# The causal mask of an SSD mixer: a triangle multiplied into the state products and a minimum on VectorE, in place of masking matmuls on TensorE

## The reference, cut to what matters

```python
seg = a_cum[..., :, None] - a_cum[..., None, :]
decay = jnp.where(causal, jnp.exp(jnp.where(causal, seg, 0.0)), 0.0)
cb = jnp.einsum('bclgn,bcsgn->bcgls', cc, bc)
y_diag = jnp.einsum('bcgrls,bcsgrp->bclgrp', cb[:, :, :, None] * decay, xdt)
```

## Time and profile before

| | us |
|---|---|
| median of 3 runs | 1277.57 |
| the runs | 1276.2 to 1277.68 |
| the profiled execution | 1276.93 |
| its span, first to last instruction | 1275.0 |
| TensorE (PE) busy in it | 1254.1 |
| VectorE (DVE) busy | 832.5 |
| ScalarE (ACT) busy | 513.0 |

### The profile page before, as it was taken

One profiled execution on the slowest core, in us unless ns is written; L12 is line 12 of the kernel. 1 busy time (PEld: TensorE's weight loads), 2 busy tenths in 40 slices (PEclk: granted clock), 3 DMA queues, 4 the chain that ended last, 5 costly groups with the idle time before them and its releaser, 6 DMA issues.

```text
span 1275.0 us, 16443 instructions
## 1 busy us (share of the span) xinstructions
PE 1254.1 (98%) x6120; PEld 1011.2 (79%) x6120; DVE 832.5 (65%) x1002; ACT 513.0 (40%) x794; POOL 234.5 (18%) x157
## 2 busy tenths in 40 slices
PE   7999999999999999999999999999999999999997
PEld 6777777777787888888878888888888888888886
DVE  4546646646397546634787777767686777787863
ACT  5435535547675225213433242424232423233441
POOL 0000000052300002610221111111111121212118
PEclk9999999999999999999999999999999999999999
DMA  6101001110004212110211211111111212111113
GB/s 244 50 34 34 33 33 34 33 50 17 1 1 149 67 67 83 66 34 4 80 67 33 67 50 49 49 49 66 39 60 57 67 39 66 33 67 33 66 58 125
DMA packets 22803, 71.93 MB, mean 56 GB/s; under 512 B 2528, under 2 KB 2784, under 8 KB 22752
## 3 DMA queue, kind: packets, MB, share of 16 engines
q1 hardware_dynamic: 22752, 71.22, 16.4%
HBM read 67.02 MB, written 4.19 MB: 56 GB/s over the span
## 4 chain that ended last, share of the span: by engine, by line
PE 68%; DVE 11%; issue 9%; ACT 5%; DMA 3%; POOL 2%; DVEq 1%; SPq 0%; ACTq 0%; POOLq 0%
PE ps L736 14%; PE ps L738 14%; PE ps L737 14%; PE ps L1095 4%; PE ps L1094 4%; PE ps L1093 4%; DVE w_lo L607 3%; DVE conv_ff L1960 2%; PE ps L831 2%; PE ps L814 2%; ACT conv_ff L1518 2%; DMA down_raw<-u_down 2%; DMA raw<-u_up 1%; PE ps L790 1%; ACT w_hi L602 1%
## 5 line engine op out<-in xcount | busy, mean ns | idle before, releaser
L736 PE MATMUL ps<-x_hi,w_hi 128*128 128x512 f32 x336 | 139.3, 414 | 8.5 <-DVE x_lo L1714 7.3
L1093 PE MATMUL ps<-mix_hi,w_hi 128*128 128x512 f32 x352 | 137.1, 389 | 0.9 <-DVE partial L1991 0.9
L1094 PE MATMUL ps<-mix_lo,w_hi 128*128 128x512 f32 x352 | 136.9, 389 | 0.0
L1095 PE MATMUL ps<-mix_hi,w_lo 128*128 128x512 f32 x352 | 136.9, 389 | 0.0
L738 PE MATMUL ps<-x_hi,w_lo 128*128 128x512 f32 x336 | 132.4, 394 | 0.0
L737 PE MATMUL ps<-x_lo,w_hi 128*128 128x512 f32 x336 | 131.9, 393 | 0.0
L2012 DVE TENSOR_TENSOR acc<-acc,ps 128x512 f32<-128x512 f32 x144 | 95.6, 683 | 42.5 <-PE ps L738 42.2
L2279 POOL TENSOR_TENSOR weight_sums<-raw 128x512 f32<-128x512 f32 x22 | 32.0, 1452 | 471.4 <-DMA raw<-u_up 471.4
L736 PE MATMUL ps<-h_hi,w_hi 128*128 128x512 f32 x288 | 113.7, 395 | 1.5 <-DVE acc L2012 0.6
L737 PE MATMUL ps<-h_lo,w_hi 128*128 128x512 f32 x288 | 112.2, 390 | 0.0
L738 PE MATMUL ps<-h_hi,w_lo 128*128 128x512 f32 x288 | 112.1, 389 | 0.0
(11 more groups left out here) (264 smaller groups left out, 2723.1 us busy)
## 6 DMA issues: line engine op xcount, KB each, us to landing
raw<-u_up SPq DMA_DIRECT2D x44, 512.0 KB, 3.3
raw<-u_in SPq DMA_DIRECT2D x22, 512.0 KB, 3.3
down_raw<-u_down SPq DMA_DIRECT2D x38, 256.0 KB, 2.7
x_stage<-u_x SPq DMA_DIRECT2D x8, 512.0 KB, 8.8
raw<-u_out SPq DMA_DIRECT2D x8, 512.0 KB, 3.3
x_nat<-x_nat SPq DMA_DIRECT2D x8, 512.0 KB, 3.3
raw<-u_gate SPq DMA_DIRECT2D x8, 512.0 KB, 3.2
out<-o_norm SPq DMA_DIRECT2D x7, 512.0 KB, 2.6
```

Source lines behind the costliest of these rows:

```text
L736: mm(dst, w_hi, x_hi, start=first, stop=False)
L1093: mm(dst, w_h[:, k], t_h[:, kt, :], start=fresh and kt == 0, stop=False, skip_group_check=True)
L1094: mm(dst, w_h[:, k], t_l[:, kt, :], start=False, stop=False, skip_group_check=True)
L1095: last = mm(dst, w_l[:, k], t_h[:, kt, :], start=False, stop=kt == 3, skip_group_check=True)
```

## The change

The mask leaves TensorE: `mask(h)` and its two tables are gone, and so is the wait of `between(h)` for it. In its place `products(g)` multiplies `cb<g>` by a triangle of ones while it takes it out of PSUM, and it does so on VectorE, not on ScalarE. `decayed(h)` takes the minimum of `decayed` and one before the product with `cb`, so that an exponential above the diagonal can't spoil the zero. VectorE's order around the stage is written anew. `TASKS` and `PAIR_OF` stay as they are. Two small VectorE instructions that made the tables at the kernel's start go too.

```diff
-MASK_BEFORE = {"cu1": 0, "st2": 1, "cb1": 2, "yy0": 3}
-MASK_INSIDE = {4: 4, 6: 5}
...
-        def mask(h):
-
-            eng.wait_ge(cexp_done, h + 1)
-            dst = two(task_place("cu%d" % h)[0])
-            for b in range(2):
-                last = mm(dst[:, b * HALF:(b + 1) * HALF].rearrange("p (k n) -> p k n", k=4), ident_r[:, :],
-                          mask_r[:, :].unsqueeze(1).broadcast_to([P, 4, P]), start=False, stop=True, skip_group_check=True)
-            last.then_inc(masked, 1)
...
-        def products(g):
-            src, free = task("cb%d" % g)
-            act(cb[:, g, :], src, ACT.Copy).then_inc(free, 1)
...
-            act(ce[h][:, :], src, ACT.Exp).then_inc(cexp_done, 1)
+            act(ce[h][:, :], src, ACT.Exp)
...
             src, free = task("cu%d" % h)
-            eng.wait_ge(masked, h + 1)
...
-        products(0)
         between(1)
         from_start(2)
         between(2)
-        products(1)
...
+        def products(g):
+            src, free = task("cb%d" % g)
+            by_tile = lambda ap: ap.rearrange("p (k n) -> p k n", k=MT)
+            v.tensor_tensor(by_tile(cb[:, g, :]), by_tile(src), table("tri_le").unsqueeze(1).broadcast_to([P, MT, P]),
+                            ALU.mult).then_inc(free, 1)
...
-            v.tensor_tensor(wt[h][:, :], wt[h][:, :], cb[:, g, :], ALU.mult)
+            v.scalar_tensor_tensor(out=wt[h][:, :], in0=wt[h][:, :], scalar=1.0, in1=cb[:, g, :],
+                                   op0=ALU.min, op1=ALU.mult)
...
                 attended_low(0)
-                attended_low(1)
+                products(0)
...
+        decayed(0)
+        decayed(1)
+        attended_low(1)
         attended_low(2)
-        for h in range(6):
+        decayed(2)
+        products(1)
+        for h in range(3, 6):
             decayed(h)
```

More of the change, by code:

```diff
@@ L321, in build @@
     un_b = put("weights_t1", [P, HALF], F32, top[0] - 4 * HALF)
-    mask_r = put("mask", [P, P], F32R)
     zero = put("zero", [P, 1])
@@ L325, in build @@
     cap_gt = put("cap_gt", [P, P])
-    ident_r = put("ident_r", [P, P], F32R)
     pool_w = put("pool_w", [P, 2, P])
@@ L451, in build @@
     decay_done = sem("decay_done")
-    cexp_done, masked, wt_done = sem("cexp_done"), sem("masked"), sem("wt_done")
+    wt_done = sem("wt_done")
     xdt_done = sem("xdt_done")
@@ L929, in _ @@
                 others(eng)
-            if name in MASK_BEFORE:
-                mask(MASK_BEFORE[name])
             if kind == "cu":
@@ L960, in _ @@
                     last = mm(dst[:, c * P:(c + 1) * P], col.broadcast_to([P, P]), table("tri_le"),
-                              start=c % 4 == 0, stop=False, skip_group_check=True)
+                              start=c % 4 == 0, stop=c % 4 == 3, skip_group_check=True)
             elif kind == "bt":
@@ L981, in _ @@
                 for c in range(MT):
-                    if i == 0 and c in MASK_INSIDE:
-                        mask(MASK_INSIDE[c])
                     t = slice(c * P, (c + 1) * P)
@@ L1723, in _ @@
         link(v.tensor_scalar(cap_gt[:, :], table("cap_le"), -1.0, NEG / SCALE, ALU.mult, ALU.max))
-        v.tensor_copy(ident_r[:, :], table("ident"))
-        v.tensor_scalar(mask_r[:, :], table("cap_le"), 0.0, 32768.0, ALU.min, ALU.mult)
         for it in PROLOGUE[:4]:
```

## The result

The changed kernel takes 1283.87 us (median of 6 runs, 1282.99 to 1285.22) against 1276.80 in the runs of before beside it (6 runs, 1275.66 to 1277.68): ratio 1.0057, 95% interval 1.0047 to 1.0067, slower. The profiled execution took 1283.81, its span 1281.8.

A forecast was written before the change was run, and what follows sets the result against it. The prediction took VectorE to bound the SSD stage, up to the start of `rm0`. A wait of 4.1 us plus 1.55 for TensorE's clock gave 5.65, so 1283.2 us against 1277.57, range 1280.3 to 1285.4.

The forecast's parts named there:

- The masks, worth nothing: SSD stage, TensorE: twelve masking matmuls, some 3.6 us, leave an engine that waits at the stage's end; counted at nothing.
- The first products in the place of `attended_low(1)`, nothing: VectorE before the last states: `products(0)` takes the split's place at ordinary length 1.2 us, so the states end as before.
- The minimum, nothing: VectorE's `decayed(h)`: the form with a minimum costs no more than the plain product, at most 0.3 us on the path.
- `cu5` behind the second product: TensorE: `cu5` waits 6.5 us for banks that `products(1)`, starting at 368.67, must read; `rm0` comes 4.1 us later.
- The clock: TensorE: clock falls to half inside the 6.5 us gap, `cu5` takes 3.35 us; adds 1.55, bounds 0 and 1.8.
- One of the two readings: Trace evidence for the clock's fall: matmul spacing 0.43 against 0.24 at the start, and granted clock 0.52 after the end.
- The two chains meet at 388.5: End of the stage: TensorE's own queue from `cu5` and VectorE's chain to `rm0` both end at 388.5.
- Nothing behind `rm0`: After the stage: nothing gives the delay back; VectorE's output-weight splits shift with it and TensorE is busy to the end.
- The sum: Whole kernel: the wait's 4.1 plus the clock's 1.55 us make it 5.65 us slower; chance 0.55.
- later still: Rival: longer half-speed stretch, dearer product out of PSUM or wider VectorE spacing, one to three us more; chance 0.10.
- the clock stays up: Rival: TensorE's clock doesn't fall in the gap before `cu5`, so only 4.1 us, 1281.7; chance 0.22.
- faster: Rival: TensorE sets `rm0` after all and the stage shortens by 3.6 us of masks, 1274.0; chance 0.04.

The follow-up runs named there:

- best order: Changed kernel with `products(0)` before `attended_low(0)`, `products(1)` behind `decayed(0)`, `between(4)` before `from_start(5)`, `gated(1)` before `pool_low(0)`: 1278.61 us, 1.0015 of before.
- products early: Changed kernel with VectorE's `products(1)` moved up behind `decayed(0)`, heads 1 and 2 behind the two splits: 1280.59 us, 1.0031 of before.
- gap filled and the exponentials swapped: Changed kernel with 28 idle matmuls ahead of `cu5` and ScalarE's `between(4)` ahead of `from_start(5)`: 1279.67 us, 1.0022 of before.
- exponentials swapped alone: Changed kernel with only ScalarE's `between(4)` put ahead of `from_start(5)`: 1282.76 us, 1.0052 of before.
- filled gap: Changed kernel with 28 unread 128x128 matmuls on TensorE while `cu5` waits: 1280.58 us, 1.0034 of before.

## Why the prediction was right, point by point

*The masks, worth nothing*: right. Alone they gave 0.2 us of the stage, and the waits before `cb1` and `rm0` grew by 1.7.

*The first products in the place of `attended_low(1)`, nothing*: right. The first split still takes 2.68, the product behind it 1.21, and `cb1` starts 20.66 us behind `xt1` in both profiles. In the best order, where the split stands behind the product, away from GpSimd, it took 1.22; this may be a part of the 1.5 us by which that order's stage is shorter than that of the products early.

*The minimum, nothing*: right, 1216 ns and a ratio of 1.0001. By the sentence of the Trainium skill on this form ("Vector Engine (DVE) Microarchitecture Reference", section "Points that are easy to get wrong") that kernel would be up to 6.8 us slower, an estimate from six at 1.135; its interval ends at 1.4.

*`cu5` behind the second product*: right in place and size. Idle 6.53 for 6.5; the product at 368.25, on the clock of before's stage 368.68 for 368.67. The wait without the clock came to +4.12, forecast 4.1.

*The clock*: right in kind, the size at the upper end. I took 1.55, with bounds of 0 and 1.8; measured 1.7 to 1.8 (5.8 and 5.9, less 4.12). `cu5` to `yy0` took 3.68 us (369.62 to 373.30), not 3.35: full half speed. And the slow clock lasted to 374, so that it cost TensorE's queue 2.2 us in this profile: 18.8 from `cu5` to `rm0`, against 16.6 with the gap filled and the exponentials swapped (with the exponentials swapped alone it is 18.3). One of the two readings behind the forecast was weaker than it looked: at the kernel's start the windows view gives a granted clock of 1.00 from 7 us on, so the 1.2 GHz there rests on the spacing of the matmuls alone.

*The two chains meet at 388.5*: right. `rm0` has no idle time in the one profile of the changed kernel and 0.32 in the other. The swap and the filling show it from both sides: either one alone frees only what the other chain allows.

*Nothing behind `rm0`*: wrong by about a microsecond. The text said that nothing gives time back; I hadn't thought that something could take more. The step that failed is the sentence "Behind `rm0` nothing gives it back ... and TensorE is busy to the end", taken as a sum of zero. TensorE wasn't without waits there even before: between 600 and 1215 us they are 1.7 in all (0.9 for `partial`, 0.6 for `acc`, 0.2 for `w_lo`), and 2.4 in the changed kernel. What stands in place of the zero: 0.8 us in the loop, with a wait of 1.22 us near 785 that before doesn't have. That this wait comes from a weight transfer that meets a load of instructions is argued, as said above.

The sum was 5.65; measured 5.92 in the stage, 0.8 in the loop and 0.1 left over, 6.8 in the spans and 7.07 in the medians. The forecast of 1283.2 stood 0.7 under 1283.87, and that it is no more is in part luck: it was built on 1277.57 for the kernel before, and the runs beside the changed kernel gave 1276.80. The change itself was forecast 1.4 too small, 0.3 of it in the stage and the rest behind it. The ratio of 0.996 in the prediction is before over after; the 1.0057 above is after over before. In the rival "later still", one to three us more than 1283.2 is 1284.2 to 1286.2, not 1284.5 to 1286.5; nothing rests on it. The rival "the clock stays up" is what the filled gap measured, +3.9 us for 4.1. The rival "faster" fails on its own point: eight instructions stood ahead of the product.

## What to carry to other kernels

When a copy out of PSUM moves to another engine, look up who takes its banks next and what stands behind that task on its queue: this change lost 5.9 us in its stage with an instruction that itself costs 1.2, and moving it up by six places gave two thirds of that back. Work taken off an engine that waits at the end of the stage turns into waiting time, however busy the page says it is. A gap in TensorE's work can be paid twice, once as a wait and once at 1.2 GHz; some idle matmuls in it (ten here, 2.4 us of rows) are a cheap test of the second part.

## What the runs showed of the hardware that I had not expected

- The granted clock fell to 0.50 with far less than a stop of 6.5 us: in the best order the only waits of over 0.25 us from 343 to 370 were 1.52 us before `cb1` and 2.38 before `yy0`, and it was at 0.50 in the window 368 to 370. With the same order and the wait filled, where it stayed at 1.00, the stage was 1.0 us shorter. In the kernel without masks but with the products on ScalarE, waits of 1.52, 0.74 and 1.51 us left it at 1.00.
- A transfer of 512 KB into whose data a load of instructions of 16 KB fell landed after 4.7 to 5.1 us, not 3.1 to 3.4 (eight profiles and six). Ten matmuls more on TensorE moved that load by 2.7 us against the weights, so two kernels that differ at 365 us can differ by a microsecond near 780. That the load delays the transfer is argued from this, not shown by moving the load alone.
- A split of 1024 columns on VectorE took 2.68 us beside GpSimd and 1.22 alone, in the same stage.
